# Two attentions of a fused two-model kernel: probabilities turned by a product with a diagonal of inverse sums

## What is computed

```python
# C, first model
m = jnp.maximum(jnp.max(logits, axis=-1, keepdims=True), sink)
e = jnp.exp(logits - m)
den = jnp.sum(e, axis=-1, keepdims=True) + jnp.exp(sink - m)
p = (e / den).astype(vb.dtype)
o = jnp.einsum('bkgqs,bskd->bqkgd', p, vb)
...
# second model
s = jnp.einsum('bqhd,bkhd->bhqk', q_nope, k_nope) + jnp.einsum('bqhr,bkr->bhqk', q_rope, k_rope)
p = jax.nn.softmax(s.astype(jnp.float32) * SOFTMAX_SCALE, axis=-1).astype(v.dtype)
return jnp.einsum('bhqk,bkhd->bqhd', p, v)
```

## Time and profile before

| | us |
|---|---|
| median of 3 runs | 3419.76 |
| the profiled execution | 3418.59 |
| its span | 3416.8 |
| first transposition to last, first model | 221.6 to 342.8 and 1122.5 to 1242.9 |
| the same, second model | 1897.8 to 2105.8 and 2817.1 to 2974.6 |

### The profile page before, as it was taken

How to read it: one execution, slowest core, us unless ns; L and a number is a source line. 1 busy time by engine, 2 the same in 40 slices (tenths; PEclk the granted TensorE clock), 3 DMA queues, 4 the chain that set the end, 5 groups by cost and what they waited for, 6 DMA issues and landing times.

```text
span 3416.8 us, 53567 instructions
## 1 busy us (share of the span) xinstructions
PE 3349.6 (98%) x20066; PEld 2771.9 (81%) x20066; DVE 2071.2 (61%) x3301; ACT 1368.7 (40%) x2172; POOL 161.5 (5%) x39
## 2 busy tenths in 40 slices
PE   8999999999999999999999999999999999999998
PEld 6766888888877578888889777988888988888887
DVE  7876457444679745655567655664444676565546
ACT  6556333222364553322222555352332346644323
POOL 2320000000033010000000000000000000000000
PEclk9999999999999999999999999999999999999999
DMA  4235332222222543332221001111111210123222
GB/s 146 87 142 206 111 123 103 95 98 98 87 99 99 188 159 123 111 119 99 99 97 64 26 26 46 62 62 64 70 65 62 73 63 26 58 75 110 88 98 86
DMA packets 45783, 317.14 MB, mean 93 GB/s; under 512 B 5008, under 2 KB 7312, under 8 KB 8464
## 3 DMA queue, kind: packets, MB, share of 16 engines
q1 hardware_dynamic: 44720, 307.07, 25.0%
q10 hardware_dynamic: 864, 7.31, 0.5%
HBM read 312.26 MB, written 2.10 MB: 92 GB/s over the span
## 4 chain that ended last, share of the span: by engine, by line
PE 85%; DVE 8%; ACT 2%; issue 2%; DVEq 1%; DMA 0%; POOL 0%; ACTq 0%; SPq 0%; POOLq 0%
PE psum L848 23%; PE psum L849 23%; PE psum L854 23%; PE psum L1518 3%; PE psum L1555 2%; PE psum L1539 2%; DVE MA L2603 1%; PE psum L934 1%; PE psum L997 1%; DVE S L2552 1%; PE psum L1481 1%; PE psum L956 1%; DVE xn L2447 1%; PE psum L1483 1%; DVE top L2583 1%
## 5 line engine op out<-in xcount | busy, mean ns | idle before, releaser
L848 PE MATMUL psum<-xh,whi 128*128 128x512 f32 (+1 forms) x2224 | 853.8, 386 | 3.8 <-issue 1.6
L849 PE MATMUL psum<-xl,whi 128*128 128x512 f32 (+1 forms) x2224 | 847.6, 383 | 0.0
L1757 ACT ACTIVATE whi<-wst 128x2048 fp32r<-128x2048 f32 x229 | 437.5, 1910 | 540.0 <-PE psum L854 527.5
L2349 DVE TENSOR_TENSOR wlo<-wst,whi 128x2048 fp32r<-128x2048 f32 x197 | 451.3, 2291 | 165.2 <-ACT whi L1757 163.0
L854 PE MATMUL psum<-xh,wlo 128*128 128x512 f32 (+1 forms) x2224 | 536.3, 383 | 0.1
L848 PEld LDWEIGHTS psum<-xh,whi 128*128 128x128 f32 x2224 | 418.0, 188 | 95.7 <-issue 14.5
L849 PEld LDWEIGHTS psum<-xl,whi 128*128 128x128 f32 x2224 | 418.1, 188 | 81.2 <-issue 1.0
L854 PEld LDWEIGHTS psum<-xh,wlo 128*128 128x128 f32 x2224 | 409.9, 188 | 82.2 <-POOL wlo L813 0.5
L813 POOL TENSOR_TENSOR wlo<-wst,whi 128x2048 fp32r<-128x2048 f32 x34 | 160.7, 4728 | 1083.1 <-ACT whi L1757 1082.8
L848 PE MATMUL psum<-uh,whi 128*128 128x512 f32 x480 | 186.9, 389 | 0.0
L849 PE MATMUL psum<-ul,whi 128*128 128x512 f32 x480 | 186.7, 389 | 0.0
(11 more groups left out here) (419 smaller groups left out, 5864.2 us busy)
## 6 DMA issues: line engine op xcount, KB each, us to landing
wst<-weights SPq DMA_DIRECT2D x287, 1024.0 KB, 4.8
dft<-c_dft ACTq DMA_DIRECT2D x2, 2688.0 KB, 9.0
hT<-x_t SPq DMA_DIRECT2D x4, 512.0 KB, 9.1
wst<-weights SPq DMA_DIRECT2D x2, 512.0 KB, 6.7
cT<-ctx_t ACTq DMA_DIRECT2D x1, 1024.0 KB, 6.8
out<-hT SPq DMA_DIRECT2D x1, 1024.0 KB, 4.9
out<-hT SPq DMA_DIRECT2D x2, 512.0 KB, 3.7
masks<-c_masks SPq DMA_DIRECT2D x1, 644.0 KB, 12.4
```

The lines of the kernel that those rows point to most:

```text
L848: pe.matmul(out, weights(m.whi, k), head(k), start=opens and n == 0, stop=False)
L849: pe.matmul(out, weights(m.whi, k), tail(k), start=False, stop=False)
L1757: act.activation(m.whi[:, slot, :], m.wst[:, slot, :], ACT.Copy).then_inc(s.hi_ready, 1)
L2349: TT(m.wlo[:, slot, :], m.wst[:, slot, :], m.whi[:, slot, :].bitcast(F32), ALU.subtract).then_inc(s.lo_ready, 1)
```

## The change

TensorE's `turn` no longer transposes. It multiplies the same block of S, as the stationary operand, by a diagonal matrix that holds 1/den of the block's head; the result is the transposed block with its columns already divided. VectorE builds the two diagonals of a unit (both heads, 128 by 256) from the identity and rden, right behind the reciprocal, and `turn` waits for them in place of the exponentials. Two diagonal buffers a model alternate; a diagonal waits for the products that read its buffer two units ago.

The products that spread the sums are gone, and so is ScalarE's copy to Rs. `normalized` is a plain copy out of bank 6. On VectorE the reciprocals now stand ahead of the next unit's maxima, and in the first model `normalized` stands behind them. On ScalarE in the first model both exponentials of the next unit now stand ahead of all copies of this one; before, they alternated.

The diff, cut to its core:

```diff
--- before.py
+++ after.py
@@ -507,13 +507,15 @@
         m.S4, at = place(nc, at, "S4", [P, 4, 4 * P])
         m.PT, at = place(nc, at, "PT", [P, 5, 4 * P])
         m.rows, at = place(nc, at, "rows", [P, 256])
-        m.Rs, at = place(nc, at, "Rs", [P, 2, P])
+        diag0, at = place(nc, at, "diag0", [P, 2, P])
         m.den, at = place(nc, at, "den", [P, 8])
         m.top8, at = place(nc, at, "top8", [P, 3, 8])
         m.cs, at = place(nc, at, "cs", [P, KT, 64])
         m.rstd, at = place(nc, at, "rstd", [P, T])
         m.rtok, at = place(nc, at, "rtok", [P, QB])
         m.warm, at = place(nc, at, "warm", [P, 1])
+        diag1, at = place(nc, at, "diag1", [P, 2, P])
+        m.diag = diag0, diag1
         assert at <= 229376, at
         m.R, _ = place(nc, work, "R", [P, 2, T])
         m.xs, _ = place(nc, work + 4096, "xs", [P, 2, T])
...
@@ -604,6 +606,8 @@
         ko0_area = v_area + 4 * 6 * 2 * HG * VH
         ko0, _ = place(nc, ko0_area, "ko0", [P, TA])
         m.Ko = ko0, ko1
+        diag2_1, _ = place(nc, ko0_area + 4 * TA, "diag2_1", [P, 2, P])
+        m.diag2 = diag2_0, diag2_1
         m.Koh = [place(nc, area, f"koh{i}", [P, TA], F32R)[0] for i, area in enumerate((ko0_area, ko1_area))]
         m.Kol, at = place(nc, region, "Kol", [P, 2, TA], F32R)
         qol0, _ = place(nc, at, "qol0", [P, T], F32R)
...
@@ -928,11 +931,12 @@
             def turn(l, u, c):
 
                 (br, qb, i), at = UNITS[u], RING["T", u, c]
-                pe.wait_ge(s.exp_ready, 2 * (l * N_UNITS + u + 1))
+                pe.wait_ge(s.diag_ready, l * N_UNITS + u + 1)
                 bank = ring_bank(l, at)
                 for b in range(4 * c, min(4 * c + 4, blocks_of(u))):
-                    last = pe.transpose(ps[bank][:, (b % 4) * P:(b % 4 + 1) * P],
-                                        scores(u, b % 2)[:, (b // 2) * P:(b // 2 + 1) * P], ident)
+                    last = pe.matmul(ps[bank][:, (b % 4) * P:(b % 4 + 1) * P],
+                                     scores(u, b % 2)[:, (b // 2) * P:(b // 2 + 1) * P], m.diag[u % 2][:, b % 2, :],
+                                     start=True, stop=True)
                 last.then_inc(s.t_done, 1)
 
             def values(u, par):
@@ -976,15 +980,6 @@
                                    start=b < 2, stop=b >= n - 2)
                     if b % 4 >= 2 or b >= n - 2:
                         mm.then_inc(s.pv_done, 1)
-
-            def denominators(l, u):
-
-                pe.wait_ge(s.rden_ready, l * N_UNITS + u + 1)
-                for par in range(2):
-                    c = 2 * (u % 4) + par
-                    last = pe.matmul(ps[6][HD * par:HD * (par + 1), P:2 * P], m.rden[:, c:c + 1].broadcast_to([P, HD]),
-                                     ident, start=True, stop=True)
-                last.then_inc(s.rs_done, 1)
 
             def rows_of(l, k):
 
@@ -1054,8 +1049,6 @@
                         weighted(l, u - 1)
                     for c in range(2, chunks_of(u) if u < N_UNITS else 0):
                         turn(l, u, c)
-                    if u:
-                        denominators(l, u - 1)
                     if (ADA_AT.get(u - 1, 0) + 1) % GATHER == 0:
                         columns_of(l, ADA_AT[u - 1] // GATHER)
                     if u and u in ADA_AT:
@@ -1532,12 +1525,13 @@
                     if u == 0:
                         pe.wait_ge(s.p2_dve, projected_by(BY_DVE, l, 0, None))
                         pe.wait_ge(s.p2_act, projected_by(BY_ACT, l, 0, None))
-                    pe.wait_ge(s.exp2_ready, 2 * (unit0 + u + 1))
+                    pe.wait_ge(s.diag2_ready, unit0 + u + 1)
                     bank = ring_bank(at)
                     for b in range(4):
                         kb = 2 * c + b // 2
-                        last = pe.transpose(ps[bank][:, b * P:(b + 1) * P],
-                                            m.S2[:, 2 * (u % 2) + b % 2, kb * P:(kb + 1) * P], ident)
+                        last = pe.matmul(ps[bank][:, b * P:(b + 1) * P],
+                                         m.S2[:, 2 * (u % 2) + b % 2, kb * P:(kb + 1) * P], m.diag2[u % 2][:, b % 2, :],
+                                         start=True, stop=True)
                     last.then_inc(s.t2_done, 1)
 
                 def weighted(u):
@@ -1557,15 +1551,6 @@
                                        start=b < 2, stop=b >= n - 2)
                         if b % 4 >= 2:
                             mm.then_inc(s.pv2_done, 1)
-
-                def denominators(u):
-
-                    pe.wait_ge(s.rden2_ready, unit0 + u + 1)
-                    for par in range(2):
-                        c = 2 * (u % 4) + par
-                        last = pe.matmul(ps[6][VH * par:VH * (par + 1), P:2 * P],
-                                         m.rden2[:, c:c + 1].broadcast_to([P, VH]), ident, start=True, stop=True)
-                    last.then_inc(s.r2_done, 1)
 
                 for n in range(4):
                     project(0, n)
...
@@ -1781,7 +1765,7 @@
                 (br, qb, i), unit = UNITS[u], l * N_UNITS + u
                 width = blocks_of(u) // 2 * P + (1 if br == "C" else 0)
                 if unit >= 4:
-                    act.wait_ge(s.rden_ready, unit - 3)
+                    act.wait_ge(s.diag_ready, unit - 3)
                 act.wait_ge(s.max_ready, 2 * unit + par + 1)
                 sc = scores(u, par)[:, 0:width]
                 act.activation(sc, sc, ACT.Exp, bias=m.nmax[:, 2 * (u % 2) + par:2 * (u % 2) + par + 1], scale=-1.0,
@@ -1797,14 +1781,6 @@
                         act.wait_ge(s.pv_done, 2 * (chunk - 4 if CHUNK0[u] + c >= 5 else l * CHUNKS1))
                     act.activation(m.PT[:, (CHUNK0[u] + c) % 5, 0:w], ps[4 + at % 2][:, 0:w], ACT.Copy
                                    ).then_inc(s.t_copied, 1)
-
-            def denominators(l, u):
-
-                unit = l * N_UNITS + u
-                act.wait_ge(s.rs_done, unit + 1)
-                if unit >= 2:
-                    act.wait_ge(s.o_ready, unit - 1)
-                act.activation(m.Rs[:, u % 2, :], ps[6][:, P:2 * P], ACT.Copy).then_inc(s.rs_copied, 1)
 
             def modulation(l, u):
 
@@ -1945,14 +1921,10 @@
                         next_split(SL_C + 1, TL_C + 2)
 
                 for u in range(N_UNITS + 1):
-                    for par in range(2):
-                        if u and u + 1 < N_UNITS:
-                            exponential(l, u + 1, par)
-                        if u < N_UNITS:
-                            half = (chunks_of(u) + 1) // 2
-                            copies(l, u, range(half, chunks_of(u)) if par else range(half))
-                    if u:
-                        denominators(l, u - 1)
+                    for par in range(2 if u and u + 1 < N_UNITS else 0):
+                        exponential(l, u + 1, par)
+                    if u < N_UNITS:
+                        copies(l, u, range(chunks_of(u)))
                     modulation(l, u)
                     if u in SPLIT_AT:
                         split(*slab_of(SL_MERGE + SPLIT_AT[u], l, SLABS1), tile0 + TL_C + 6)
...
@@ -2192,14 +2164,6 @@
                     if chunk >= 5:
                         act.wait_ge(s.pv2_done, 2 * (chunk - 4))
                     act.activation(m.PT2[:, chunk % 5, :], ps[4 + at % 2][:, :], ACT.Copy).then_inc(s.t2_act, 1)
-
-                def denominators(u):
-
-                    unit = unit0 + u
-                    act.wait_ge(s.r2_done, unit + 1)
-                    if unit >= 2:
-                        act.wait_ge(s.o2_ready, unit - 1)
-                    act.activation(m.Rs2[:, u % 2, :], ps[6][:, P:2 * P], ACT.Copy).then_inc(s.r2_copied, 1)
 
                 def spectra(numbers):
 
...
@@ -2557,19 +2519,25 @@
             def reciprocals(l, u):
 
                 dve.wait_ge(s.exp_ready, 2 * (l * N_UNITS + u + 1))
-                nc.vector.reciprocal(m.rden[:, 2 * (u % 4):2 * (u % 4) + 2], m.den[:, 2 * (u % 4):2 * (u % 4) + 2]
-                                     ).then_inc(s.rden_ready, 1)
+                rden = m.rden[:, 2 * (u % 4):2 * (u % 4) + 2]
+                nc.vector.reciprocal(rden, m.den[:, 2 * (u % 4):2 * (u % 4) + 2])
+                dve.drain()
+                if u >= 2:
+                    dve.wait_ge(s.t_done, l * RING1 + RING["T", u - 2, chunks_of(u - 2) - 1] + 1)
+                elif l:
+                    dve.wait_ge(s.t_done, l * RING1)
+                TT(m.diag[u % 2][:, :, :], ident.unsqueeze(1).broadcast_to([P, 2, P]),
+                   rden.unsqueeze(2).broadcast_to([P, 2, P]), ALU.mult).then_inc(s.diag_ready, 1)
 
             def normalized(l, u):
 
                 br, qb, i = UNITS[u]
                 dst = {"A": m.OA, "B": m.OB, "C": m.OC}[br]
                 dve.wait_ge(s.pv_done, 2 * (l * CHUNKS1 + CHUNK0[u + 1]))
-                dve.wait_ge(s.rs_copied, l * N_UNITS + u + 1)
                 into = dst[:, i, qb * P:(qb + 1) * P]
```

(28 more changed lines are left out.)

7 lines of the change are left out of this document (2 added, 5 removed).

## The result

The changed kernel takes 3539.4 us (median of 4 runs, 3538.46 to 3540.59) against 3419.6 for the kernel before (median of 4 runs, one more than in the section on the time before): ratio 1.035, 95% interval 1.0332 to 1.0368, slower by 120 us. The forecast was 3517, the range 3490 to 3544: the time lies in the range, 22 us above the forecast.

A forecast was written before the change was run, and what follows sets the result against it. Attention was taken to run at TensorE's pace. The profiled 3418.6 us, plus 85.2 net on TensorE and 12 of waits, gave 3516; lying 1.2 under the median, it became 3517 us, range 3490 to 3544.

The forecast's parts named there:

- The exchange on TensorE: In the turns, 984 transpositions become two-record products, 0.226 us a block against 0.110: +114 us (103 to 128).
- Rival 2: In the turns, the new product costs four transpositions, 0.44 us a block: 3727 us; chance 3%.
- The spread products: On TensorE, the two products that spread the sums go, 0.22 us a unit for 132 units: -29.0 us.
- Waits: TensorE waiting where the diagonal lengthens a chain, at three places in attention: +12 us (-5 to +25).
- The wait from short to long: Second model, layer 0, six passages from a short unit to a long one: 0.87 us each, 5 us (0 to 8).
- 10 to 20 long units: Long units without slack now, whose slack shrinks by 0.4 us: 4 us (-5 to +9).
- Rival 3: Every unit waits for reciprocal and diagonal on top of TensorE's growth, 86 us: 3591 us; chance 7%.
- Rival 4: In attention, the 26.7 us without TensorE work fill up, leaving +58: 3478 us; chance 6%.
- the 3 us for C: C of the first model, 32 units where VectorE has no gap with a `select`: 0 to 8 us, taken as 3.
- The entries "at nothing": The four first turns of an attention wait for a diagonal, +0.6 us each; offset by the last units, left at nothing.
- No change of clock: In the four attention windows, the granted clock is 1.00, its upper level of 2.4 GHz, and expected to stay.
- Rival 1: In the turns, a product with a diagonal passes as one record, the exchange is free: 3402 us, faster; chance 4%.

The follow-up runs named there:

- experiment 1: The kernel before, with an ordinary product by the identity in place of the transposition, nothing else changed: 3507.9 us, ratio 1.027.
- experiment 6: The changed kernel, with the second model's diagonals ahead of `normalized` and the first model's first diagonal ahead of the last rotation: 3498.9 us, ratio 1.0237.
- Experiment 4: The changed kernel, with the second model's reciprocal and diagonal of the next unit ahead of the waiting `normalized` on VectorE: 3502.5 us, ratio 1.0248.
- Experiments 5 and 8: The changed kernel, first model: unit 0's reciprocal and diagonal ahead of the last rotation, 3535.0 us; then unit 1's too, its exponentials ahead of ScalarE's swap, 3534.4 us.
- Experiment 2: The changed kernel, with turns transposing by the identity again but still waiting for the diagonal, division by the sums left out: 3455.3 us, ratio 1.0106.
- experiment 7: The changed kernel with the second model's diagonals and the first model's first diagonal moved earlier, S and diagonals rounded to fp32r: 3431.1 us, ratio 1.0034.
- experiment 5: The changed kernel, with the first model's unit 0 reciprocal and diagonal ahead of the last rotation: 3535.0 us, ratio 1.0339.

## Why the prediction held, and which steps did not

- **The exchange on TensorE: right.** 0.113 us a record was taken, 0.111 measured; +114 against +111. It lies between the two bounds, 0.107 by the columns and 0.11 to 0.12 by the weight loads, at the lower loads' value; no run tells which of the two sets it. The rule of the Trainium skill (TensorE: Matmul & The Clock Gate, section Terms: transposition four times faster for FP32) doesn't hold for this kernel: 0.2225 / 0.110 = 2.0 times, in the changed kernel and in experiment 1. Rival 2 is out.
- **The spread products: right.** Their lines are gone. The product by itself brings +89 with them still there (experiment 1), and with no more idle time than before the whole change brings +81 (experiment 6), where its net was put at +85.
- **Waits: mis-sized.** I said +12 us with +25 as the upper end. The time has 120 - 82 = 38 us beyond TensorE's net work of 111 - 29. My own mark for this step, 25 us more in front of the turns than 14.5, was passed: it is 31.3 more. The reckoning priced the diagonal at its own length, and asked what stands *behind* the reciprocal on VectorE. It never asked what stands *ahead* of it, though the order showed `normalized` as the last row of the piece quoted there, just ahead of the next unit's reciprocal. The wait from short to long was sized right where it was looked for: 0.24 + 0.87 us was the forecast, 1.15 or 1.16 came, though five times and not six. The "10 to 20 long units" at +0.4 us are what was wrong: 36 units wait in all, for up to 2.6 us. Experiment 4 moves that one thing and takes 36.9 us out of the second model.
- **Rival 3, the diagonal in the open: partly so.** Its mechanism is the one that came, with 32.7 us in the second model and 13.1 in the first of the 86 it was given, and not in every unit.
- **Rival 4, the growth half covered: hidden by the above.** Alone (experiment 1) the product does fill 18.9 of its 111 us into waits. Its 26.7 us were read from windows that hold 66 us more than the attentions; from first turn to last TensorE was idle for 24.1 us, which moves this rival's sum by 3 us and the forecast by nothing.
- **The first model's units: right.** +27.6 us in two stretches, against 28.9 with the 3 us for C.
- **The entries "at nothing": wrong.** The first model's two cost 6.9 us. In the text each was charged a diagonal's length, but the diagonal stands behind a rotation that waits for ScalarE. Experiments 5 and 8 show that a fix is not had by moving one or two diagonals; that VectorE's fixed row of work at the entry is the reason fits them and was not tested by itself.
- **"No change of clock": wrong.** The mean went from 0.999 (before, only the last 6 us are lower, and TensorE has no work there) to 0.995. TensorE's busy time grew by 98.9 us, 17 over the net work of 82; in experiment 6, where the second model's long waits are gone and the record counts are the same, it grew by 84.1. The lower clock is only part of these 15 us. At half speed 18.4 busy us can have cost 9 at most, and in experiment 6 3.4 us of the attentions are at 0.50, 2 at most: some 7 us, an estimate from these windows. Another part may be that each wait leaves the last record in front of it with its full length of 0.28 us in the busy time, where the pace is 0.11; this was not measured.
- **Rival 1: its sum was wrong, though not its verdict.** It said that a product as cheap as a transposition would give 3402 us. Experiment 2 has that and gives 3455. So a block at 0.127 us would not have been the point at which the change breaks even.

So the time came inside the range because the exchange, by far the largest term, was right. The waits stood outside their own bounds, at 38 us against 25. That the sum still fell inside is in part luck: the range's upper end had room for a dearer exchange (128 us), and the missed waits used it up.

## What to carry to other kernels

When a change makes an engine wait for a new producer, read the producer's own row upwards too: whatever waits ahead of it there is added to the new wait, and moving the producer by one place can be worth much even if no work changes (here 36 waits of up to 2.6 us became 8 of up to 1.2, and 37 us of 120 went). Price an exchange of one product for another by the records that each leaves and by the pace of the chain, and try it alone: here the forecast from the chain's rows was within 3%. At the entry of the first model a wait that was taken away came back at the engine's next inputs, and gave next to nothing.

## What was not expected of the hardware

- An f32 product of 128 by 128 with fp32r operands leaves one record and keeps 0.10 us (experiment 7), under the 0.110 us of an f32 transposition by the identity; the full f32 product keeps 0.2225 us with two records.
- The granted clock fell to its lower level at a single stretch of 3.95 us without work, for 6.8 us, and at one of 2.63 us, for 3.4; nowhere in the attentions of the kernel before did it leave 1.00. In experiment 1, where TensorE hardly waits, the windows from 220 to 230 stay at 1.00 although its product is as long. The same wait of 2.67 us at the same place was followed by a lower clock in experiment 5 and by none in experiment 6, so such a wait does not always bring the clock down.
